# Down projections of two feed-forwards as seven products of quarters instead of eight, in a two-layer float32 kernel

## The chip, the cores and the metric

The kernel runs on one core of one Trainium2 chip. The metric is the device time of one execution in microseconds (us), as the median over runs. Engines are named PE (TensorE, the matmuls), DVE (VectorE), ACT (ScalarE), POOL (GpSimd) and SP (SyncE, whose queue starts all the DMAs of this kernel).

## The reference, cut to what matters

Two transformer layers follow each other on 1024 tokens of width 1024, all in float32. Each ends in a feed-forward with 2816 hidden units, which is 22 blocks of 128:

```python
# first layer (hybrid_layer)
gu = jnp.einsum('bsd,df->bsf', x, w_gu)
gate, up = gu[..., :FFN_HIDDEN], gu[..., FFN_HIDDEN:]
ffn = jnp.einsum('bsf,fd->bsd', jax.nn.silu(gate) * up, w_down)
return layer_norm(DEEPNORM_ALPHA * x + ffn, ln2_g, ln2_b)
# second layer (second_block)
h = rmsnorm(x, g_ffn_pre[l]) * (1.0 + scale_f) + shift_f
f = (jax.nn.silu(h @ w_gate[l]) * (h @ w_up[l])) @ w_down[l]
x = x + gate_f * rmsnorm(f, g_ffn_post[l])
```

What is at issue here is the last product of each, hidden (1024 tokens x 2816) times `w_down` (2816 x 1024). Before the feed-forward of the first layer stand three mixers (a gated one, a differential attention with 4 heads, a sparse attention whose keys are the top 256 of a score) and an output projection; before that of the second a stick-breaking attention and a pooling mixer. A vector of modulations for the second layer, silu(c) times `w_cond_2` (1024 x 6144), is computed beside the first layer's feed-forward.

## The kernel before, in words

**Precision.** A float32 operand x is held as two numbers of a shorter form, high and low: ACT copies x into `wh` (or `yh`), and POOL (for weights) or DVE (for activations) subtracts it from x into `wl` (or `yl`). Each product of two blocks is three matmuls, high x high, high x low and low x high, added up in one bank of PSUM (L546 to L548 for the down projections, L1878 to L1880 for gate and up). A matmul has a 128x128 stationary part and 512 columns that stream.

**Weights.** All weights come in units of 128x1024 numbers (512 KB) in one fixed order, `plan`. SP loads them into a ring of 3 buffers `raw` (L430), ACT and POOL split them into a ring of 5 pairs `wh`, `wl` (L478, L481 and L493, L498). `ahead(m)` says how many loads and splits may have been issued by the time unit m is used; `sp_feed`, `act_feed`, `pool_feed` issue up to that point, and each engine's queue runs strictly in order.

**The feed-forward of a layer** (`pe_ffn`, `act_ffn`, `pool_ffn`, `dve_ffn`, `sp_ffn`, called once per layer) has three stages:
- Early: the first 4 of the 22 hidden blocks, gate and up, as plain products (L520 to L522).
- Pairs: the other 18 blocks, 2 at a time, first gate (even q), then up (odd q). With tokens, inputs and columns halved, each q is a product of 2x2 quarters, which Strassen's scheme in Winograd's form makes from 7 products instead of 8: 18 x 7 products s of 12 matmuls. DVE makes the four sums of weights (`wdiff`, L460 to L465) and puts the 7 products together from the banks (L2011, L2020, L2022); for odd q it multiplies by the silu of the gate (L2018). The finished pair of hidden blocks lies in one of two buffers `hid`, and SP stores it to `qk_d` in DRAM, 2 transfers of 512 KB for each odd q (L2119). `BESIDE_LAST` brings the first 6 blocks back during the last pair. In the first layer DVE also adds up one part of the modulations in most products (L1675; its 256 KB of `w_cond_2` come through the buffers `early`, SP, L1685), and PE turns sums of 8 parts (L1645).
- Down: the 22 hidden blocks come back from DRAM in 4 chunks (`CHUNKS`: 6, 6, 6 and 4 blocks). For each chunk, each half n of the output columns and each block tb of 128 tokens, one bank takes 18 (or 12) matmuls, and DVE adds it to `res`, which holds all 1024x1024 outputs (L2069, L2075, L2077). That is 22 x 16 x 3 = 1056 matmuls per layer. The last chunk goes tb by tb, so that the norm behind it starts block by block (`after_block`, `after_half`). In the first layer `res` starts as the residual, which SP brings back once `res` is free (`sp_residual`).

**The attention of the first layer** (`pe_attend` and its like, 48 events and 7 places behind them) ran with no weights to feed: eight units of `w_out` were loaded beforehand and five of them split. DVE finishes the choice of keys (L1195 to L1209) and then takes maxima and sums for PE's logits (L1322, L1347).

Banks are handed out by rings; `ring(*bufs)` gives a new ring, and `prior(key)` is what freed a bank last.

## Time and profile before

| what | value |
|---|---|
| median of 3 runs | 2487.4 us (2480.76 to 2490.2) |
| the profiled execution | 2484.37 us |
| its span in the profile | 2482.2 us, 31284 instructions |
| PE busy | 2376.1 us (96%), 11999 matmuls |
| DVE, ACT, POOL busy | 1495.6, 962.7, 671.6 us |
| the chain that ended last | PE 79%, DVE 11%, DMA 4%, ACT 3%, issue 1%, POOL 1% |
| memory read and written | 197.36 and 59.82 MB, 104 GB/s over the span |

The stages of the feed-forwards in the trace: early 666 to 757 us, pairs 757 to 1122, down 1122 to 1373 in the first layer; early 1797 to 1889, pairs 1889 to 2233, down 2233 to 2474 in the second. The first layer's attention takes 345 to 574. A matmul's duration in the trace (389 ns) is that of one instruction from start to end; since several are under way at once, what counts is the distance from one start to the next.

### The profile page before, as it was taken

Reading aid. Unit: us, or ns where it says so; the run is one execution under the profiler, and the core shown is the slowest. Engines: PE = TensorE matmul, PEld = TensorE weight load, DVE = VectorE, ACT = ScalarE, POOL = GpSimd, SP = SyncE. Lnnn points to the kernel's source line nnn. Section 1 sums busy time; section 2 is a strip of 40 time slices with the busy share of each in tenths; the row PEclk is TensorE's granted clock in tenths of the full one; section 3 lists DMA queues with packets and bytes.
Section 4 is the critical chain, followed back from the end, with each engine's and each line's share of the span. In section 5 each row is a group of like instructions: output and inputs, shape, how many; then the busy total and the mean of one; then the engine's idle time right before and its main releaser. Section 6 shows DMA issues by size and latency. Waiting matters only on the chain.

```text
span 2482.2 us, 31284 instructions
## 1 busy us (share of the span) xinstructions
PE 2376.1 (96%) x11999; PEld 1922.5 (77%) x11999; DVE 1495.6 (60%) x2510; ACT 962.7 (39%) x1834; POOL 671.6 (27%) x382
## 2 busy tenths in 40 slices
PE   8999978889999999999999999999899999999998
PEld 6678866777888777777888777777688888888886
DVE  3588998662776777854226578773674555453225
ACT  3467837771222322232212355563533223231212
POOL 3013210000233545542222321110223445442220
PEclk9999988999999999999999999999999999999999
DMA  5026451214314454545332210001421322243333
GB/s 177 9 64 191 153 178 56 98 31 154 122 55 140 149 161 145 168 163 192 102 106 90 71 52 27 28 26 69 144 77 57 96 86 69 85 144 111 102 111 119
DMA packets 219980, 259.21 MB, mean 104 GB/s; under 512 B 16540, under 2 KB 150188, under 8 KB 219832
## 3 DMA queue, kind: packets, MB, share of 16 engines
q1 hardware_dynamic: 219832, 257.22, 31.7%
q8 instruction: 95, 1.56, 0.3%
q14 instruction: 53, 0.43, 0.1%
HBM read 197.36 MB, written 59.82 MB: 104 GB/s over the span
## 4 chain that ended last, share of the span: by engine, by line
PE 79%; DVE 11%; DMA 4%; ACT 3%; issue 1%; POOL 1%; SPq 0%; POOLq 0%; DVEq 0%; ACTq 0%
PE bank L546 10%; PE bank L548 10%; PE bank L547 10%; PE bank L1878 7%; PE bank L1879 7%; PE bank L1880 7%; PE bank L520 6%; PE bank L521 6%; PE bank L522 6%; PE bank L1387 2%; PE bank L2512 1%; DMA early<-in_w_cond 1%; DVE res L1322 1%; PE bank L2481 1%; PE bank L565 1%
## 5 line engine op out<-in xcount | busy, mean ns | idle before, releaser
L498 POOL TENSOR_TENSOR wl<-raw,wh 128x1024 fp32r<-128x1024 f32 x117 | 298.3, 2566 | 1333.0 <-ACT wh L481 1312.9
L546 PE MATMUL bank<-wh,yh 128*128 128x512 f32 x704 | 277.9, 395 | 5.5 <-DVE sum3l L1843 2.8
L547 PE MATMUL bank<-wl,yh 128*128 128x512 f32 x704 | 275.3, 391 | 0.0
L548 PE MATMUL bank<-wh,yl 128*128 128x512 f32 x704 | 275.3, 391 | 0.0
L481 ACT ACTIVATE wh<-raw 128x1024 fp32r<-128x1024 f32 x117 | 123.1, 1060 | 308.5 <-PE bank L548 291.5
L493 POOL TENSOR_TENSOR wl<-res,wh 128x512 fp32r<-128x512 f32 x144 | 197.9, 1397 | 151.0 <-ACT wh L478 130.3
L1878 PE MATMUL bank<-yh,wh 128*128 128x512 f32 x576 | 225.2, 391 | 0.0
L1880 PE MATMUL bank<-yh,wl 128*128 128x512 f32 x576 | 224.2, 389 | 0.0
L1879 PE MATMUL bank<-yl,wh 128*128 128x512 f32 x576 | 224.1, 389 | 0.0
L493 POOL TENSOR_TENSOR wl<-raw,wh 128x512 fp32r<-128x512 f32 x108 | 157.6, 1474 | 228.6 <-ACT wh L478 228.6
L520 PE MATMUL bank<-yh,wh 128*128 128x512 f32 x448 | 180.2, 402 | 8.3 <-DVE yl L583 8.3
L2077 DVE TENSOR_TENSOR res<-bank,res 128x512 f32<-128x512 f32 x96 | 65.6, 689 | 190.8 <-PE bank L548 190.7
L2011 DVE TENSOR_TENSOR res<-bank,res 128x512 f32<-128x512 f32 x144 | 99.6, 692 | 131.1 <-PE bank L1880 123.2
L522 PE MATMUL bank<-yh,wl 128*128 128x512 f32 x448 | 175.3, 391 | 0.0
L521 PE MATMUL bank<-yl,wh 128*128 128x512 f32 x448 | 175.1, 391 | 0.0
L546 PEld LDWEIGHTS bank<-wh,yh 128*128 128x128 f32 x704 | 133.0, 189 | 35.7 <-issue 4.6
L478 ACT ACTIVATE wh<-res 128x512 fp32r<-128x512 f32 x144 | 83.4, 623 | 194.7 <-DVE res L465 145.2
L548 PEld LDWEIGHTS bank<-wh,yl 128*128 128x128 f32 x704 | 132.9, 189 | 27.9
L547 PEld LDWEIGHTS bank<-wl,yh 128*128 128x128 f32 x704 | 133.1, 189 | 27.0
L1878 PEld LDWEIGHTS bank<-yh,wh 128*128 128x128 f32 x576 | 108.1, 188 | 29.8 <-issue 4.3
L1880 PEld LDWEIGHTS bank<-yh,wl 128*128 128x128 f32 x576 | 108.1, 188 | 22.7
L1879 PEld LDWEIGHTS bank<-yl,wh 128*128 128x128 f32 x576 | 108.1, 188 | 22.2
(345 smaller groups left out, 5385.9 us busy)
## 6 DMA issues: line engine op xcount, KB each, us to landing
early<-in_w_cond SPq DMA_DIRECT2D x96, 256.0 KB, 3.0
raw<-in_w_gu SPq DMA_DIRECT2D x44, 512.0 KB, 4.1
raw<-in_w_down SPq DMA_DIRECT2D x44, 512.0 KB, 3.6
raw<-in_w_in SPq DMA_DIRECT2D x40, 512.0 KB, 4.1
qk_d<-res SPq DMA_DIRECT2D x36, 512.0 KB, 4.2
raw<-in_w_gate SPq DMA_DIRECT2D x22, 512.0 KB, 4.2
raw<-in_w_up SPq DMA_DIRECT2D x22, 512.0 KB, 4.2
res<-in_x SPq DMA_DIRECT2D x16, 512.0 KB, 9.8
```

Of the source, the lines that this page charges most:

```text
L481: act.i.activation(wh[n % NU][:, :], raw_of(u)[:, :], ACT.Copy).then_inc(*av.up(("wh", u)))
L493: pool.i.tensor_tensor(wl[n % NU][:, half], src, wh[n % NU][:, half].bitcast(F32), ALU.subtract).then_inc(*po.up(("wl", u)))
L498: pool.i.tensor_tensor(wl[n % NU][:, :], raw_of(u)[:, :], wh[n % NU][:, :].bitcast(F32), ALU.subtract).then_inc(*po.up(("wl", u)))
L520: pe.i.matmul(bank[:, :], a, a_h[:, s], start=k == 0, stop=False)
L521: pe.i.matmul(bank[:, :], a, a_l[:, s], start=False, stop=False)
L522: last = pe.i.matmul(bank[:, :], b, a_h[:, s], start=False, stop=k == 7)
L546: pe.i.matmul(bank[:, 0:wide], xa, h[:, c:c + wide], start=k == 0, stop=False)
L547: pe.i.matmul(bank[:, 0:wide], xa, l[:, c:c + wide], start=False, stop=False)
L548: last = pe.i.matmul(bank[:, 0:wide], xb_, h[:, c:c + wide], start=False, stop=k == nk - 1)
L1878: pe.i.matmul(bank[:, :], h[:, c:c + 128], high[:, k, :], start=k == 0, stop=False)
L1879: pe.i.matmul(bank[:, :], h[:, c:c + 128], low[:, k, :], start=False, stop=False)
L1880: last = pe.i.matmul(bank[:, :], l[:, c:c + 128], high[:, k, :], start=False, stop=k == 3)
```

## The change

The same scheme of seven products now makes the down projection of the 18 later blocks. They go as 9 couples (blocks 2c and 2c+1 of them), which are the two halves of the inner dimension; the tokens are halved at 512 and the output columns at 512. The hidden side needs 7 operands for each couple, 4 as they are and 3 sums, all 128x512: DVE makes one (`third`), POOL the other three (`pool_parts`) right behind each odd q, and SP stores all seven (256 KB each) to `parts_d`. The weight side needs 7 operands too; three are quarters of `w_down`, and four are sums ("crossed weights"). These are made ahead: for the first layer by POOL beside the attention (`pool_cross`, 9 x 4 subtractions of 128x512, in the place of two of the `raw` buffers), for the second by DVE in odd q of its pairs (`dve_cross`, 9 x 4), each time loaded (1 MB) and stored (1 MB) by SP.

The down stage (`pe_down`) then runs 7 products, one after the other. A product i holds four banks open at once, one for each 128 of the 512 tokens, and goes over its 9 couples; an operand (i, c) is one 256 KB transfer of hidden numbers and half a unit "D" of weights, and serves 4 x 3 matmuls. 20 slots take the operands; SP loads 16 ahead, ACT and DVE split 8 ahead. DVE puts the products together in `res` with two sums `u_sum` and `v_sum` (`dve_down`). The 4 early blocks follow as plain products, tb by tb, as the last chunk did before. In matmuls: 7 x 9 x 4 x 3 + 4 x 16 x 3 = 756 + 192 = 948 per layer, where 1056 were.

```diff
-CHUNKS = [(0, 6), (6, 6), (12, 6), (18, 4)]
+N_EARLY, N_PAIR, N_COUPLE = 4, 18, 9
+N_OPERAND, N_HIDDEN, N_SLOT = 63, 71, 20
...
-            for a, k in CHUNKS:
-                for n in range(2):
-                    units += [("T", wd, j, 512 * n) for j in range(a // 2, (a + k) // 2)]
+            units += [("D", layer, i) for i in range((N_OPERAND + 1) // 2)]
+            for n in range(2):
+                units += [("T", wd, j, 512 * n) for j in range(N_EARLY // 2)]
...
+        def pool_cross():
+            for c in range(N_COUPLE):
+                pool.wait_ge(*cross_in[0].after(c))
+                for out_, x, y in cross(1):
+                    pool.wait_ge(*po.now())
+                    pool.i.tensor_tensor(out_, x, y, ALU.subtract).then_inc(*po.up(("cross", 1, c)))
...
         def sp_attend():
...
             for t in range(N_PLACES):
+                if t % 5 == 1 and t // 5 < N_COUPLE:
+                    sp_cross_in(1, t // 5)
+                if t % 5 == 4 and t // 5 < N_COUPLE:
+                    sp_cross_out(1, t // 5, po)
+                if t == 5 * N_COUPLE:
+                    sp.wait_ge(*cross_out[0].after(N_COUPLE - 1))
+                    sp_feed(project_released(N_PROJECT - 1))
...
+        LOAD_BESIDE = {0: range(0, 4), 1: range(4, 8), 2: range(8, 12), 4: range(12, 16), 5: range(16, 17)}
+        SPLIT_BESIDE = {3: range(0, 2), 4: range(2, 4), 5: range(4, 5), 6: range(5, 8)}
+        LOADS_AHEAD, SPLITS_AHEAD = 16, 8
...
+        def pool_parts(layer, q):
+
+            a11, a21, a12 = piece(q, 0, 0), piece(q, 0, 1), piece(q, 1, 0)
+            pool.wait_ge(*dv.after(("part", layer, 3, q)))
+            pool.i.tensor_tensor(a21, a11, a21, ALU.subtract).then_inc(*po.up(("part", layer, 4, q)))
+            pool.wait_ge(*dv.after(("hidden", layer, q, 6)))
+            pool.i.tensor_tensor(whole, third, a11, ALU.subtract).then_inc(*po.up(("part", layer, 2, q)))
+            pool.wait_ge(*po.now())
+            pool.i.tensor_tensor(first[1], a12, whole, ALU.subtract).then_inc(*po.up(("part", layer, 6, q)))
...
+            G["r"] = ring(*banks)
+            for i in range(7):
+                pe_down(layer, i)
+            G["r"] = ring(*banks[0:5])
...
+        def pe_down(layer, i):
+
+            for t in range(4):
+                key = ("down product", layer, i, t)
+                G["r"].open(key)
+                pe.wait_ge(*G["r"].prior(key))
+            for c in range(N_COUPLE):
+                o = N_COUPLE * i + c
+                u = down_unit(layer, o)
+                pe.wait_ge(*dv.after(("operand", layer, o)))
+                h, l = pe_unit(u)
...
+                for t in range(4):
+                    bank = uses.held["down product", layer, i, t]
+                    xa, xb_ = high[:, 128 * t:128 * t + 128], low_[:, 128 * t:128 * t + 128]
+                    pe.i.matmul(bank[:, :], xa, h[:, cols_], start=c == 0, stop=False)
+                    pe.i.matmul(bank[:, :], xa, l[:, cols_], start=False, stop=False)
+                    last = pe.i.matmul(bank[:, :], xb_, h[:, cols_], start=False, stop=c == N_COUPLE - 1)
...
+            if q % 2 and s == 5:
+                dve_part(layer, q)
             if s == 3:
+                dve.wait_ge(*part_stored(3, q // 2 - 1).after((layer, 3, q // 2 - 1)))
+                dve.wait_ge(*po.after(("part", layer, 2, q // 2 * 2 - 1)))
                 dve.i.tensor_tensor(third, bank[:, :], u, ALU.add).then_inc(*dv.frees(uses, key))
...
+                    if layer == 2 and q % 2 and s == 0:
+                        dve_cross(q // 2)
...
                 for s in range(7):
...
+                    if q and q % 2 == 0 and s in (0, 1):
+                        for i in ((4,), (2, 6))[s]:
+                            sp_part(layer, i, q - 1)
...
                     if layer == 1:
                         sp_mod(q, s)
+                    if q % 2:
+                        for i in {1: (0,), 4: (5,), 5: (3,), 6: (1,)}.get(s, ()):
+                            sp_part(layer, i, q)
...
+            for o in range(N_OPERAND):
+                dve_operand(layer, o + SPLITS_AHEAD)
+                if o % N_COUPLE == N_COUPLE - 1:
+                    dve_down(layer, o // N_COUPLE)
```

How it moves instructions is seen at three places. The first is SP's queue in the pairs of the first layer, from product s = 5 of an odd q into the even q behind it. `qk_d` and `parts_d` are the stores of the hidden numbers, `early` the loads of `w_cond`. Before:

```order
L1685 DMA early_128<-in_w_cond 128x512 [waits dve_done]
L2119 DMA qk_d<-res 128x1024
L1685 DMA early_129<-in_w_cond 128x512 [waits dve_done]
L2119 DMA qk_d<-res 128x1024
L1685 DMA early_128<-in_w_cond 128x512 [waits dve_done]
L1685 DMA early_129<-in_w_cond 128x512 [waits dve_done]
```

And now:

```order
L1758 DMA early_128<-in_w_cond 128x512 [waits dve_done]
L1918 DMA parts_d<-res 128x512
L1753 DMA vec_d<-macc_131 1x512
L1758 DMA early_129<-in_w_cond 128x512 [waits dve_done]
L1918 DMA parts_d<-res 128x512
L1918 DMA parts_d<-res 128x512 [waits pool_done]
L1758 DMA early_128<-in_w_cond 128x512 [waits dve_done]
L1918 DMA parts_d<-res 128x512 [waits pool_done] x2
L1758 DMA early_129<-in_w_cond 128x512 [waits dve_done]
```

The stores are seven smaller ones for each odd q, and three of them wait for POOL ahead of two loads of `w_cond`. The second place is POOL's queue behind an odd q, whose splits stood back to back before; now:

```order
L523 TENSOR_TENSOR wl_64<-raw_56,wh_59 128x512 [waits act_done]
L523 TENSOR_TENSOR wl_64<-res,wh_59 128x512 [waits dve_done]
L1929 TENSOR_TENSOR res<-res 128x512
L1931 TENSOR_TENSOR res<-res 128x512
L1933 TENSOR_TENSOR res<-res 128x512 [waits pool_done]
L523 TENSOR_TENSOR wl_65<-res,wh_60 128x512 [waits act_done]
L523 TENSOR_TENSOR wl_65<-res,wh_60 128x512
```

Three subtractions stand between the splits of one unit and the next. The third place is POOL's queue across the attention, where nothing stood before between the last split of `w_out` and the next stage; of the 9 groups that stand there now, the last is followed by the splits of the stage behind:

```order
L529 TENSOR_TENSOR wl_66<-raw_56,wh_61 128x1024 [waits act_done,raw_in2]
L1566 TENSOR_TENSOR cross_132<-cross_132 128x512 [waits pool_done,cross_in0]
L1566 TENSOR_TENSOR cross_132<-cross_132 128x512 [waits pool_done] x3
L1566 TENSOR_TENSOR cross_132<-cross_132 128x512 [waits pool_done,cross_in0]
L1566 TENSOR_TENSOR cross_132<-cross_132 128x512 [waits pool_done] x3
```

Each group of four waits for a load of 1 MB and works in place, so the four run one after the other.

## Rows read from the trace of the kernel before

**Rows 1.** The page, busy time of PE: us, share of the span, instructions.

```profile
PE 2376.1 (96%) x11999; PEld 1922.5 (77%) x11999; DVE 1495.6 (60%) x2510; ACT 962.7 (39%) x1834; POOL 671.6 (27%) x382
```

**Rows 2.** By stage: us, then PE, PEld, DVE, ACT, POOL busy, PEclk, DMA share, GB/s.

```profile
345.00:574.00 229.00, 181.83 (x1356) 151.77 (x1356) 166.88 (x498) 159.29 (x412) 5.10 (x2) 0.88 0.29 98
...
757.00:1122.00 365.00, 359.16 (x1538) 285.06 (x1537) 265.71 (x339) 110.22 (x183) 178.33 (x122) 1.00 0.50 156
1122.00:1373.00 251.00, 247.92 (x1096) 204.91 (x1097) 101.14 (x143) 51.64 (x66) 67.55 (x27) 0.99 0.34 119
...
1889.00:2233.00 344.00, 343.72 (x1517) 284.28 (x1515) 179.61 (x231) 111.78 (x184) 163.83 (x122) 1.00 0.29 92
2233.00:2474.00 241.00, 239.95 (x1056) 198.04 (x1056) 88.17 (x116) 46.89 (x58) 49.65 (x19) 1.00 0.33 111
```

**Rows 3.** What PE waited for: us in total, times, longest.

```profile
PE bank L1297 <- DVE st L1322: 21.9, 7, 16.6
...
PE bank L1645 <- DVE macc L1675: 5.8, 2, 3.3
PE bank L546 <- POOL wl L498: 3.2, 7, 0.7
...
PE bank L546 <- DVE sum3l L1843: 2.8, 2, 2.2
```

**Rows 4.** PE in order of time, from the first layer's pairs into its down stage.

```profile
1121.59 0.39 PE L1880 MATMUL bank<-sum4h,wl 128*128 128x512 f32 x1
1124.20 0.50 PE L546 MATMUL bank<-wh,yh 128*128 128x512 f32 x1 [2.22 <-DVE sum3l L1843]
...
1126.83 0.63 PE L547 MATMUL bank<-wl,sum2h 128*128 128x512 f32 x1
1127.25 0.63 PE L548 MATMUL bank<-wh,sum2l 128*128 128x512 f32 x1
```

**Rows 5.** Durations in ns (min/median/max) of 128x512 operations of DVE and POOL.

```profile
L2018 DVE TENSOR_TENSOR res<-res x72: 691/693/1984, 787.4 to 2239.7; 128x512 f32<-128x512 f32 x72
...
L2011 DVE TENSOR_TENSOR res<-bank,res x144: 691/692/695, 766.8 to 2239.0; 128x512 f32<-128x512 f32 x144
...
L493 POOL TENSOR_TENSOR wl<-res,wh x144: 1269/1297/1762, 740.5 to 2206.8; 128x512 fp32r<-128x512 f32 x144
```

**Rows 6.** DVE by line, whole span: count, busy us, mean ns, idle time before.

```profile
L2018 DVE TENSOR_TENSOR res<-res 128x512 f32<-128x512 f32 x72 | 66.0, 916 | 2.5
```

**Rows 7.** DVE by line, 345 to 574 us, forms together; columns as in Rows 6.

```profile
L1347 DVE SCALAR_TENSOR_TENSOR res<-res,st 128x128 f32<-128x128 f32 (+7 forms) x32 | 26.2, 819 | 1.1
...
L1440 DVE SCALAR_TENSOR_TENSOR osb<-osb,st,sg 128x128 f32<-128x128 f32 x32 | 8.8, 346 | 0.1
```

**Rows 8.** POOL in order of time, 330 to 360 us.

```profile
345.12 5.10 POOL L498 TENSOR_TENSOR wl<-raw,wh 128x1024 fp32r<-128x1024 f32 x2 [19.88 <-ACT wh L481]
```

**Rows 9.** DVE in order of time, around those two operations of POOL.

```profile
345.15 2.87 DVE L1201 SCALAR_TENSOR_TENSOR junk<-res,cand,junk 128x512 bf16<-128x512 f32 x1
348.06 2.71 DVE L1205 SCALAR_TENSOR_TENSOR score<-score,cand,junk 128x512 f32<-128x512 f32 x1
350.80 0.69 DVE L1209 SCALAR_TENSOR_TENSOR score<-score,nd 128x512 f32<-128x512 f32 x1
...
353.64 0.88 DVE L1201 SCALAR_TENSOR_TENSOR junk<-res,cand,junk 128x640 bf16<-128x640 f32 x1
```

**Rows 10.** What DVE waited for, 757 to 1122 us: us in total, times, longest.

```profile
DVE macc L1675 <- DMA early<-in_w_cond: 27.9, 23, 5.1
DVE res L2011 <- PE bank L1880: 22.9, 22, 4.7
DVE macc L1672 <- DMA vec_d<-macc: 20.6, 4, 5.9
```

**Rows 11.** DMA issues: operation and count, KB each, median us from issue to landing.

```profile
early<-in_w_cond SPq DMA_DIRECT2D x96, 256.0 KB, 3.0
```

**Rows 12.** The fastest 5 us of transfers in the first down stage, columns as in Rows 2.

```profile
1140.00:1145.00 5.00, 5.00 (x24) 4.13 (x23) 0.00 (x0) 0.00 (x0) 0.00 (x0) 1.00 1.03 415
```

424 lines of the change are left out of this document (251 added, 173 removed).

## The prediction

> **What bounds the kernel now.** I read the page first: PE is busy 2376.1 of 2482.2 us [rows 1], so the time is PE's work plus its few gaps. The table by stage says where [rows 2]: in the pairs of the second layer and in both down stages PE is busy all but 0.3 to 3.1 us, at a granted clock of 0.99 to 1.00. DVE, ACT and POOL are busy less than half of a down stage. Three places are less clean. In the first layer's attention PE is busy 181.8 of 229 us. In the first layer's pairs 365 us pass for the same products that take 344 us in the second; the modulations are made beside them, and DVE is busy 265.7 us. Third, PE pays a little at the entry of a down stage. The list of PE's waits puts numbers on them [rows 3]: 21.9 us for DVE's maxima (16.6 in one piece), 5.8 us for sums of modulations, 3.2 and 2.8 us for splits of weights and hidden numbers. So matmuls taken out of a down stage come off the time, if nothing else in that stage becomes longer than the shorter PE work, and the preparations elsewhere must not widen the gaps there.
>
> **The price of a matmul.** The second layer's down stage has 1056 of them in 239.95 us [rows 2]: 0.2272 us each. Its durations are not the price, since they overlap.
>
> **PE's work.** Per layer 1056 - 948 = 108 matmuls go, 216 in both, of the same shape. 216 x 0.2272 = **-49.1 us**. Nothing else is on PE's path in these stages, so all of it counts, provided that the rest keeps up:
>
> - One operand is 12 matmuls, 2.73 us. Per operand DVE splits 128x512 (0.69 us, as a subtraction of that size [rows 5]) and POOL half a unit (1.30 us [rows 5]). ACT copies both; it was busy 46.9 us in the stage before [rows 2], with 22 hidden blocks and 22 units per layer, and now has 35.5 of each, some 76 us of about 215. DVE adds 4 to 12 combining operations per product of 24.5 us, at most 12 x 0.69 = 8.3 us beside 6.2 us of splits. The first layer's product with 12 is the fullest, at 60%. The splits run 8 operands (22 us) ahead and a product's four banks are needed again only after the next product. I cost this at nothing. If POOL and DVE hold each other up, the cover is those 22 us.
> - Transfers: 256 KB of hidden numbers and 256 KB of weights per 2.73 us is 192 GB/s. The trace moved 119 and 111 GB/s in these stages [rows 2] but 415 GB/s over 5 us of one of them [rows 12]. In the first layer 4 MB of residual come on top, about 10 us at that rate, against the 16 operands (44 us) of loads ahead. Nothing, with 0 to +5 us for the range.
> - SP's queue issues two transfers per operand instead of one per block and one per unit. It waits for a slot freed 4 operands earlier and is far ahead of its use. Nothing.
>
> **The entry of a down stage.** Before, PE stood 2.2 us for the low half of hidden blocks and then ran at a distance of 0.42 us between matmuls for a while [rows 4]. Now it waits for the last banks of the pairs, one combining operation of 0.69 us [rows 5], while the first operands are split three products earlier. A gap of about 1 us stays, the slow stretch may too. I take 0 with -5 to +3 us for both layers.
>
> **The crossed weights of the first layer.** 36 subtractions of POOL at 1.30 us [rows 5], 47 us, run between some 360 and 540 us, where POOL did nothing. They cost through DVE. When POOL's two splits ran at 345.12 us [rows 8], DVE operations with two inputs in SBUF took 2.87 and 2.71 us, and 0.69 and 0.88 us for the same size or a larger one behind them [rows 9]; each lost about 2 us to one POOL operation of 2.55 us. Operations that read a bank never did this: 695 ns at most in 144 [rows 5]. So what counts are DVE's two-input operations here: 32 and 32 [rows 7] and some 15 for the choice of keys. In the pairs, with POOL busy 48% of the time [rows 2], one such operation took 916 ns on average against a median of 693 [rows 5, 6], 0.22 us more. Here POOL will be busy about 25% of the time, so 0.12 us x 79 = 9 us of DVE's time. DVE is on the path for part of this stage only (21.9 us of waits, most before 383 us), and the groups start there back to back. I take **+6 us**. Below it could be 0; above, each POOL operation hits one of DVE on the path: 36 x 1.3 x 0.8 = 37 us. The value is near the low end, since that is where the average over 72 operations puts it. Where the three last units of `w_out` are loaded, at place 45 of 55, some 40 us are left until the stage behind needs them. Nothing.
>
> **The seven operands beside the pairs, first layer.** POOL's 27 subtractions (35 us) fit in its queue: the splits behind them are 5 units, 10 products, ahead. DVE's 9 additions of 0.69 us do too. The place that costs is SP's queue. Behind an odd q POOL must first split a unit whose second half is a difference that DVE makes only after that q's last product: combine, multiply, part, then three of the differences, about 5 us, then ACT, the split and one subtraction, some 8 us after PE has left that q; the other two subtractions end near 11 us. SP waits for them ahead of two loads of `w_cond`, which it issued at about 6 and 9 us before. A load lands 3.0 us after its issue [rows 11], so the part of product s = 2 has its numbers about 2 us late, and that of s = 4 about as much. DVE already waits 27.9 and 20.6 us for such transfers here and only 22.9 us for PE [rows 10], so its slack is thin, but it has the rest of 14 products to catch up, and PE waits for DVE directly only at the sums of 8 parts, 5.8 us so far [rows 3]. Nine times 2 to 4 us would be 18 to 36 us if all of it reached PE. I take **+5 us**, nearer to the low end because of those 5.8 us; below 0.
>
> **The same in the second layer, and its crossed weights.** 45 more operations of DVE at 0.69 us are 31 us in a stage where DVE is busy 179.6 of 344 us and PE had 0.3 us without work [rows 2]. There are no loads of `w_cond`. **+1 us**, 0 to +3.
>
> **The sum** against the profiled execution: 2484.4 - 49.1 + 0 + 6 + 5 + 1 = 2447.3 us. The median of the runs shown is 3.0 us above that execution, so the median should be about **2450 us**.
>
> **Rivals.**
>
> *PE runs slow in the new loop* (slower). The new loop changes the bank every three matmuls, where 12 to 18 went to one bank before. If PE paused at these changes and the clock fell to its lower level, a matmul would cost 0.42 us as in the short stretch after the entry [rows 4] instead of 0.227. All 1896 at that level would be +366 us. It decides from 49.1 / 0.193 = 254 slow matmuls on, 13% of them; half of the product loops' 1512 slow gives 2450 + 146 = 2596 us. Against it: bank changes every 12 matmuls in the second layer's pairs leave the clock at 1.00 and no gap [rows 2], and nothing in the new loop waits between its groups of three. Chance 0.03. The Trainium skill (TensorE: Matmul & The Clock Gate, "A second HAM failure mode: psum-queue depth-cycling") reports a kernel whose cycling through banks in each iteration made PE idle briefly between groups, so that its clock went up and down. By that rule this rival would be the forecast; the row on the pairs, which cycle banks too, speaks against it.
>
> *Transfers starve the down stages* (slower). The products need 63 x 0.524 = 33.0 MB per layer. At the 119 GB/s seen there [rows 2] that takes 278 us instead of 172, +106 per layer: 2660 us. It decides once the rate stays below some 168 GB/s, where 25 us per layer are lost again. For it: transfers of 2 KB rows, half of them from memory that was just written. Against: 415 GB/s [rows 12]. Chance 0.03.
>
> *The first layer's pairs become paced by DVE and SP.* 4 us for each of the 9 odd q and what the locks add reach PE: +31 over my +5, 2481 us. For it: the thin slack [rows 10]. Chance 0.07.
>
> *POOL's subtractions sit on the attention's path.* +20 over my +6: 2470 us, up to 2481 at the bound. For it: DVE is the bound at the start of that stage. Chance 0.10.
>
> **How the numbers follow.** My forecast has 0.77. The range: the low end is 2487.4 - 49.1 with the entries gained, and nothing lost, 2433, of which I take 2436; the high end takes in the attention rival and the other upper bounds that may come together, to 2476. About 2 in 10 stay outside, with the two slow rivals, the pairs' rival and some of my own case. 0.5% is 12.4 us, about what a measurement of this kernel can tell from no change; below 2475 counts as faster. Faster: 0.77 and most of the attention case, 0.86. Same: the pairs' rival and the rest, 0.08. Slower: 0.06.
>
> **What would show it.** In the trace after: down stages of about 215 to 220 us each with PE busy in all but 1 or 2 us, 948 matmuls at 0.227 us, and 190 GB/s. In the attention, L1347 with a mean above 819 ns and the stage 229 us plus 4 to 10. In the first layer's pairs, longer waits of DVE for `early` and 365 us plus 2 to 8; in the second layer's, 344 to 346. POOL's three subtractions should end 9 to 12 us after the odd q. The prediction is wrong if a down stage has gaps in PE or a clock below 0.95, or if either preparation stage grows by over 15 us.

## The result and the profile after

The changed kernel takes 2498.95 us (median of 7 runs, 2496.6 to 2503.59), the kernel before 2481.59 us in the same session (7 runs): a ratio of 1.0065, 95% interval 1.005 to 1.0079. It is **slower**, by 17.4 us between the medians, where a median of 2450 us was forecast. The page of the profiled execution (2496.6 us; its span is 2494.8) answers to [rows 1]:

```profile
span 2494.8 us, 31779 instructions
...
PE 2341.4 (94%) x11783; PEld 1888.7 (76%) x11783; DVE 1680.2 (67%) x2646; ACT 1018.9 (41%) x1960; POOL 851.4 (34%) x500
...
HBM read 244.55 MB, written 92.85 MB: 135 GB/s over the span
...
PE 71%; DVE 16%; DMA 5%; POOL 3%; ACT 2%; issue 2%; SPq 0%; DVEq 0%; ACTq 0%; POOLq 0%
```

The matmuls did go: 11999 - 11783 = 216 records, and PE is busy 34.7 us less. Yet PE's share of the chain fell from 79 to 71%. Something else now sets the end in several places. The table by stage, columns as in [rows 2]: attention, pairs and down of the first layer, pairs and down of the second.

```profile
345.00:586.00 241.00, 183.58 (x1357) 151.53 (x1355) 183.20 (x497) 159.09 (x413) 57.98 (x38) 0.88 0.49 174
768.00:1164.00 396.00, 370.26 (x1540) 290.48 (x1538) 268.63 (x347) 107.39 (x185) 210.00 (x146) 0.96 0.51 159
1171.00:1379.00 208.00, 205.84 (x900) 169.96 (x901) 158.98 (x163) 71.10 (x107) 86.14 (x37) 0.99 0.58 201
1914.00:2258.00 344.00, 343.78 (x1517) 284.44 (x1515) 201.65 (x275) 109.15 (x186) 192.83 (x146) 1.00 0.49 162
2265.00:2486.00 221.00, 218.85 (x948) 180.33 (x947) 147.24 (x142) 75.72 (x116) 77.24 (x33) 0.98 0.54 182
```

Inside the seven products PE waits for nothing, and the stages move 182 to 201 GB/s. The pairs of the first layer are the surprise: 396 us for PE's 370, while DVE is busy 268.63 us, hardly more than the 265.71 before. PE's own busy time there grew too, from 359.16 [rows 2] to 370.26 us for the same products, at a granted clock of 0.96 where it was 1.00.

To add the stages up I took them between the first matmuls of successive stages, read from PE in order of time. The same table serves all runs below (us; "entry" is from the last matmul of the pairs to the first of the down stage, "down" from there to the next stage):

| kernel | start to out projection | pairs 1 | entry 1 | down 1 | pairs 2 | entry 2 | down 2 |
|---|---|---|---|---|---|---|---|
| before | 574.5 | 364.3 | 2.6 | 230.8 | 342.5 | 1.0 | 239.9 |
| changed | 585.9 | 394.9 | 7.3 | 208.2 | 342.5 | 7.2 | 221.3 |
| difference | +11.4 | **+30.6** | +4.7 | -22.6 | 0 | +6.2 | -18.6 |

The differences add to +11.7; with +1.0 between the first down stage and the second layer's pairs this is the spans' 12.6 to within 0.1. The medians lie 17.4 us apart, so this pair of profiles holds some 5 us less than the medians show; the changed kernel's reached the out projection early (585.9 us, where the median of thirteen profiles with the same code up to there is 589.0). What PE waited for, all of the span, answers to [rows 3]:

```profile
PE bank L1330 <- DVE st L1355: 27.0, 12, 16.6
PE bank L1718 <- DVE macc L1748: 25.7, 11, 4.5
PE bank L2010 <- DVE res L2116: 13.7, 2, 6.9
...
PE bank L577 <- DVE res L2232: 4.3, 2, 2.2
```

The sums of modulations (5.8 us before) now cost 25.7. With the 11.1 us that PE is busy longer this makes up the growth of the pairs, 31.0 us by these windows: about a third of it is not waiting but matmuls at a lower clock behind the waits. The last row is a small wait of 2.2 us in each layer, between the seventh product and the early blocks. A new and larger wait stands at both entries. Here is the first, PE and then DVE in order of time (start, duration, in brackets the idle time before and its releaser):

```profile
1163.56 0.39 PE L1959 MATMUL bank<-sum4h,wl 128*128 128x512 f32 x1
1170.89 0.76 PE L2010 MATMUL bank<-wh,yh 128*128 128x512 f32 x1 [6.94 <-DVE res L2116]
```

```profile
1158.38 0.69 DVE L1900 TENSOR_TENSOR yl<-landing,yh 128x512 fp32r<-128x512 f32 x1 [1.86 <-ACT yh L1895]
...
1162.34 2.07 DVE L1730 TENSOR_TENSOR macc<-macc 128x48 f32<-128x48 f32 x1
...
1166.45 2.05 DVE L2123 TENSOR_TENSOR res<-res 128x512 f32<-128x512 f32 x1
1168.54 0.69 DVE L1923 TENSOR_TENSOR res<-res 128x512 f32<-128x512 f32 x1
1169.15 0.69 DVE L1900 TENSOR_TENSOR yl<-landing,yh 128x512 fp32r<-128x512 f32 x1
1169.94 0.69 DVE L2116 TENSOR_TENSOR res<-bank,res 128x512 f32<-128x512 f32 x1
```

The down stage's first product asks for four banks at once, and one is that of the very last pair product. The operation that frees it (1169.94) stands in DVE's queue behind the operations of the products before it and behind splits that wait for ACT and a landing. Two operations ahead of it took 2.07 and 2.05 us; beside both POOL was splitting a weight unit (2.40 us from 1161.95, 2.35 from 1165.61). The first of the two takes 0.19 us in the kernel before, with nothing of POOL's beside it. PE's clock falls with the gap: the windows at the second entry show 1.00, 0.69, then 0.50 (the 1.2 GHz level), 0.90, 1.00.

```profile
2250.00:2257.00 7.00, 7.00 (x33) 5.79 (x32) 4.11 (x7) 4.77 (x8) 1.72 (x2) 1.00 0.98 358
2257.00:2264.50 7.50, 0.78 (x4) 0.32 (x2) 7.19 (x8) 3.22 (x5) 5.22 (x3) 0.69 1.02 395
2264.50:2269.00 4.50, 4.44 (x11) 3.51 (x12) 4.50 (x4) 0.00 (x0) 3.39 (x3) 0.50 1.05 397
2269.00:2274.00 5.00, 5.00 (x21) 4.12 (x20) 1.35 (x3) 1.12 (x2) 0.00 (x0) 0.90 0.89 332
```

In the pairs, SP's and DVE's largest waits, 768 to 1167 us:

```profile
SPq L1918 <- POOL res L1929: 57.6, 8, 7.7
```

```profile
DVE macc L1748 <- DMA early<-in_w_cond: 63.5, 25, 5.9
DVE macc L1745 <- DMA vec_d<-macc: 17.1, 4, 4.3
```

That looks like the forecast's mechanism at full size: SP waits 57.6 us for POOL ahead of loads of `w_cond`, and DVE waits 63.5 us for these (27.9 before). The experiments say that this reading names one way of several.

### The profile page after: what moved, and what is told of

It is laid out like the page before. It is cut to its first block, busy times and chain, and to the rows that moved or that the text cites. A ratio compares the mean times of both kernels' runs of the same rounds, so it can differ in the third digit from the quotient of the medians.

```text
span 2494.8 us, 31779 instructions
## 1 busy us (share of the span) xinstructions
PE 2341.4 (94%) x11783; PEld 1888.7 (76%) x11783; DVE 1680.2 (67%) x2646; ACT 1018.9 (41%) x1960; POOL 851.4 (34%) x500
## 4 chain that ended last, share of the span: by engine, by line
PE 71%; DVE 16%; DMA 5%; POOL 3%; ACT 2%; issue 2%; SPq 0%; DVEq 0%; ACTq 0%; POOLq 0%
PE bank L551 6%; PE bank L553 6%; PE bank L552 6%; PE bank L1957 5%; PE bank L1959 5%; PE bank L1958 5%; PE bank L577 5%; PE bank L578 5%; PE bank L579 5%; PE bank L2010 5%; PE bank L2012 5%; PE bank L2011 5%; DMA early<-in_w_cond 3%; PE bank L1420 2%; POOL wl L523 2%
## 5 line engine op out<-in xcount | busy, mean ns | idle before, releaser
L529 POOL TENSOR_TENSOR wl<-raw,wh 128x1024 fp32r<-128x1024 f32 (+1 forms) x145 | 356.6, 2465 | 1039.2 <-ACT wh L511 1019.2
L511 ACT ACTIVATE wh<-raw 128x1024 fp32r<-128x1024 f32 (+1 forms) x145 | 152.0, 1055 | 300.9 <-PE bank L2012 225.7
L1900 DVE TENSOR_TENSOR yl<-landing,yh 128x512 fp32r<-128x512 f32 x112 | 157.0, 1441 | 81.0 <-ACT yh L1895 81.0
L2010 PE MATMUL bank<-wh,yh 128*128 128x512 f32 x408 | 160.8, 394 | 13.7 <-DVE res L2116 13.7
L2116 DVE TENSOR_TENSOR res<-bank,res 128x512 f32<-128x512 f32 x144 | 99.6, 692 | 109.4 <-PE bank L1959 99.1
L577 PE MATMUL bank<-wh,yh 128*128 128x512 f32 x400 | 159.9, 400 | 6.3 <-DVE res L2232 4.3
L2011 PE MATMUL bank<-wl,yh 128*128 128x512 f32 x408 | 160.3, 393 | 0.0
L2012 PE MATMUL bank<-wh,yl 128*128 128x512 f32 x408 | 160.2, 393 | 0.0
L578 PE MATMUL bank<-wl,yh 128*128 128x512 f32 x400 | 157.4, 393 | 0.0
L579 PE MATMUL bank<-wh,yl 128*128 128x512 f32 x400 | 157.1, 393 | 0.0
L1748 DVE SCALAR_TENSOR_TENSOR macc<-early,cc,macc 128x512 f32<-128x512 f32 x84 | 85.5, 1018 | 70.0 <-DMA early<-in_w_cond 63.5
```

What stands on the lines that cost most here:

```text
L529: pool.i.tensor_tensor(wl[n % NU][:, 0:w], raw_of(u)[:, 0:w], wh[n % NU][:, 0:w].bitcast(F32), ALU.subtract).then_inc(*po.up(("wl", u)))
L577: pe.i.matmul(bank[:, 0:wide], xa, h[:, c:c + wide], start=k == 0, stop=False)
L2010: pe.i.matmul(bank[:, :], xa, h[:, cols_], start=c == 0, stop=False)
L2011: pe.i.matmul(bank[:, :], xa, l[:, cols_], start=False, stop=False)
L2012: last = pe.i.matmul(bank[:, :], xb_, h[:, cols_], start=False, stop=c == N_COUPLE - 1)
```

## The experiments

### First group: banks, SP's stores, POOL's subtractions

**Banks.** The ring of the seven products begins with the three banks that the pairs don't use and goes on with those used longest ago; the ring behind it begins with the banks of the product before last.

```
-            G["r"] = ring(*banks)
+            k = G["r"]
+            old = [k.bufs[(k.n + j) % 5] for j in range(5)]
+            G["r"] = ring(*banks[5:8], *old)
...
-            G["r"] = ring(*banks[0:5])
+            G["r"] = ring(*old[1:5], old[0])
```

> The changed kernel, but the ring of banks for the seven products starts with the three banks that the pairs do not use and then the longest free ones, so that the first product no longer needs the bank of the pairs' last product; the ring behind it starts with the banks of the product before last. Bank theory: PE's gap of 7.3 us at each entry of a down stage came only from that one bank, freed late by DVE; the gaps fall to about 1 us, the slow stretch behind them and the 2.2 us in front of the early blocks go too: 12 to 17 us less than the changed kernel, about 2484. Rival: the operands themselves are split too late, PE waits for them instead, and no more than 4 us go: about 2496.

Measured: 2478.14 us against 2486.34 of before, ratio 0.9967 (0.9956 to 0.9978). Entries 0.2 and 0.2 us, down stages 205.8 and 216.4, with the clock at 1.00 throughout:

```profile
1169.50:1340.70 171.20, 171.20 (x757) 141.75 (x755) 134.67 (x119) 66.74 (x96) 82.26 (x36) 1.00 0.70 238
...
2253.80:2424.90 171.10, 171.10 (x757) 141.70 (x755) 121.92 (x102) 66.70 (x96) 81.83 (x36) 1.00 0.63 215
```

These two windows are the seven products of each layer; no distance between two matmuls' starts is above 0.3 us in them. The theory stands. It gave more than the 14.1 us of the gaps: another 2.4 and 4.9 us in the down stages. Of these, 1.7 and 2.6 us are the matmuls at the lower clock behind the entries. The rest lies at the early blocks. With the edit's second half the distance between the two matmuls there is 1.89 us in place of 2.54 in each layer, and in the second layer seven slow matmuls behind it (1.5 us) are gone. Its pairs (397.5) are as long as the changed kernel's. Four profiles have the change's code throughout the pairs (the changed kernel, this run and two below), and they took 394.9 to 397.5 us: a difference of 3 us in one profile is not much more than this spread.

**SP's stores later.** The three stores that wait for POOL move from the first two products of an even pair to behind the `w_cond` load of the third.

```
-                    if q and q % 2 == 0 and s in (0, 1):
-                        for i in ((4,), (2, 6))[s]:
-                            sp_part(layer, i, q - 1)
...
                         sp_mod(q, s)
+                    if q and q % 2 == 0 and s == 2:
+                        for i in (4, 2, 6):
+                            sp_part(layer, i, q - 1)
```

> The changed kernel, but SP's three stores that wait for POOL stand behind the loads of w_cond of product s = 2 of the even q, instead of ahead of those of s = 0 and s = 1. Queue theory: the loads were late because SP stood before them waiting for POOL; DVE's wait for them falls from 63.5 us back towards 28, PE's wait for the sums of parts from 25.7 towards 6, and the first layer's pairs shrink from 395 us by 20 to 28: total about 2475. Load theory (rival): DVE is late from its own added work and from being held up by POOL; the stage loses no more than 6 us: total 2493 or more.

Measured: ratio 1.008 (1.0062 to 1.0098), pairs 399.5 us. SP's wait for L1929 fell from 57.6 to 7.7 us and DVE's for `early` from 63.5 to 35.7, as expected, and the time did not fall. DVE now waited 34.8 us for `vec_d` (17.1 in the changed kernel), and 7.7 us for POOL itself. The queue theory in its simple form falls, unless the row store explains it (second group).

**Without POOL's subtractions, and without those of the attention.** Two runs that leave work out:

```
-                if o % 14 == 13:
-                    pool_parts(layer, o // 7)
```

> POOL's three subtractions behind each odd q are left out (three of the seven operands then hold other numbers), their stores stay in their places in SP's queue and wait only for DVE's last hidden quarter. Queue theory: like the run with the later stores, the first layer's pairs lose 20 to 28 us, since SP no longer waits for POOL; the rest of what this run gains beyond that one is what the subtractions cost through DVE, 0 to 6 us. Load theory: this run gains 20 us or more and the run with the later stores next to nothing.

Measured, one run: 2477.64 us, pairs 373.1. This takes out 21.8 of the 30.6 us, but two causes with them, since SP's stores don't wait for POOL either (three of the seven operands hold other numbers in this run).

```
-            pool_cross()
...
-            sp.wait_ge(*done.after(("cross", layer, c)))
+            sp.wait_ge(*(cross_in[0].after(c) if layer == 1 else done.after(("cross", layer, c))))
```

> POOL's 36 subtractions beside the attention are left out (four of the weight operands of the first layer's down projection are then plain quarters); the 1 MB loads and stores around them stay, each store waiting for its load. Lock theory: POOL's subtractions hold up DVE, and the start of the output projection comes back from 586 us to 574.5 to 577. Rival: the 18 MB of transfers and their place in SP's queue delay the heads' loads and the results' stores; the start stays at 583 or later.

Measured, one run: 2488.4 us; the out projection starts at 576.6. DVE's lines in the attention (L1380 was L1347 before the change, L1377 was L1344), in the changed kernel and then here:

```profile
L1380 DVE SCALAR_TENSOR_TENSOR res<-res,st 128x128 f32<-128x128 f32 (+7 forms) x32 | 34.8, 1088 | 1.1
L1377 DVE SCALAR_TENSOR_TENSOR st<-st,cand 128x1 f32<-128x1 f32 x32 | 11.9, 371 | 1.1
```

```profile
L1380 DVE SCALAR_TENSOR_TENSOR res<-res,st 128x128 f32<-128x128 f32 (+7 forms) x32 | 26.2, 818 | 1.1
...
L1377 DVE SCALAR_TENSOR_TENSOR st<-st,cand 128x1 f32<-128x1 f32 x32 | 7.0, 220 | 1.1
```

The transfers stayed and only POOL's 36 subtractions went, so it is they that hold DVE's operations up: 8.6 + 4.9 = 13.5 us on these two lines, of which 9 to 12 reached the out projection (576.6 against 585.9 in the changed kernel's profile and 589.0 in the median). L1380 is back at the 819 ns of [rows 7]. A marker that scatters less is the last product for the logits (L1297 before, L1330 now). It starts at 541.4 us here, at 539.9 and 540.7 in the two profiles whose attention is that of before, and at 551.2 to 554.7 in the thirteen that have the subtractions.

### Second group: is it the queue or the subtraction?

**Crosses later in the attention.**

```
-                if t % 5 == 1 and t // 5 < N_COUPLE:
-                    sp_cross_in(1, t // 5)
...
+                w = t - 12
+                if w >= 0 and w % 4 == 0 and w // 4 < N_COUPLE:
+                    sp_cross_in(1, w // 4)
```

> The changed kernel with one edit: the nine groups of crossed weights beside the first attention start at its twelfth place and come every fourth place, instead of starting at once and every fifth. Nothing is left out. Theory (GpSimd's subtractions of two SBUF operands and VectorE's operations of two SBUF operands hold each other up, and 8.5 of attention's 11.4 us were lost beside the first three groups, where VectorE ends last; later TensorE ends last): the first product of the out projection starts 6 to 10 us earlier than in the changed kernel (576 to 580 against 585.9), the total is 6 to 10 us lower, about 2491. Rival (the cost goes with the number of subtractions, wherever they stand): no shift, within 3 us of the changed kernel. Rival (the groups now end too late, and w_out's load is late): first product later than 586.

Measured: ratio 1.0053 (1.0036 to 1.007), out projection at 583.9. In thirteen profiles with the code up to there as the change has it, it starts between 585.9 and 592.1, median 589.0; so the gain is 2 to 5 us and not the 6 to 10 expected. The last product for the logits starts at 547.8 us, 3.4 to 6.9 before the thirteen and 6.4 behind the run without subtractions. L1380 still took 1046 ns on average. As far as one profile can tell, the place is worth a part of the cost, and between half and two thirds of it goes with the number of subtractions.

**Stores later and row store earlier.** As the second run above, and

```
-            if h % 8 == 7 and h > 8:
+            if h % 8 == 5 and h > 8 and h < N_PART:
                 sp_mod_row(h // 8 - 1)
```

> The changed kernel with two edits: SP's three stores that wait for GpSimd move from the first and second place of an even pair to behind the w_cond load of its third (as in the run that moved these stores alone), and the row store vec_d<-macc comes two parts earlier in SP's order (at the sixth part of a group of eight in place of the eighth). Nothing is left out. Queue theory, mended (the stores' move alone gained nothing because the row store, which VectorE's next group waits for, then stood behind them and behind a weight load that waits for GpSimd's split): macc's wait for vec_d falls from 34.8 (there; 17.1 in the changed kernel) to under 5 us, the wait for early stays near 36, the first layer's pairs take 375 to 385 us against 394.9, the total is 10 to 20 lower, about 2485. Lock theory (what costs is GpSimd's subtractions beside VectorE's work, and VectorE's waits for them): the pairs stay at 392 to 400.

Measured: ratio 1.006 (1.0045 to 1.0075), pairs 396.5. DVE's wait for `vec_d` did go; that for `early` came back at 67.2 us. A wait taken from one place turned up at the next: the mended queue theory misses too.

**SP free of POOL, POOL as it was.** The stores that waited for POOL store `third` and wait for DVE. What else relied on these stores waits for them or for POOL directly: DVE ahead of writing `third`, ACT ahead of writing `first[1]`. Three operands hold other numbers in this run too.

```
-            return (piece(q, 0, 0), piece(q, 1, 0), whole, third, piece(q, 0, 1), piece(q, 1, 1), first[1])[i]
+            return (piece(q, 0, 0), piece(q, 1, 0), third, third, third, piece(q, 1, 1), third)[i]
...
-                         3: dv.after(("part", layer, 3, q))}.get(i, po.after(("part", layer, i, q))))
+                         3: dv.after(("part", layer, 3, q))}.get(i, dv.after(("hidden", layer, q, 6))))
```

> The changed kernel with SP's three stores of an even pair left where they are, but storing the sum that VectorE made in place of the three differences that GpSimd makes, and waiting for VectorE alone; GpSimd still makes its three subtractions at the same place of its own queue (their results are not stored, so the down products' operands are not the reference's). It is the counterpart of the run without these subtractions, whose pairs took 373.1. Queue theory (SP's 57.6 us of waits for GpSimd hold back the loads of w_cond, and these VectorE): first layer's pairs 372 to 380 us, macc's wait for early near 27, total 15 to 22 lower, about 2480. Lock theory (the subtractions themselves, on GpSimd, hold up VectorE's operations of two SBUF operands): pairs stay above 388. Between: each has its share, to be read from the pairs' length between 373 and 395.

Measured: ratio 1.0074 (1.0059 to 1.0089), pairs 399.4. This is the run that decides: with no store of SP's waiting for POOL the pairs are as long as ever, and without the subtractions they are 26 us shorter. (DVE's waits for POOL come to 9.3 us in all. Its wait for `early` fell to 39.1 us, but that for `vec_d` rose from 17.1 to 33.0.) SP's waits for POOL did not go but moved. These are its waits for POOL's splits ahead of a weight load, in the changed kernel and then here:

```profile
SPq L105 <- POOL wl L523: 71.2, 25, 4.7
```

```profile
SPq L105 <- POOL wl L523: 121.4, 26, 14.5
```

The trace shows by what way. SP, POOL and DVE of this run, in order of time:

```profile
867.70 2.03 SPq L1758 DMA_DIRECT2D early<-in_w_cond  x2
877.43 1.00 SPq L459 DMA_DIRECT2D raw<-in_w_gu  x2
878.48 7.74 SPq L1758 DMA_DIRECT2D early<-in_w_cond  x4
```

```profile
864.59 1.28 POOL L523 TENSOR_TENSOR wl<-raw,wh 128x512 fp32r<-128x512 f32 x1 [9.69 <-ACT wh L507]
...
867.08 1.74 POOL L1929 TENSOR_TENSOR res<-res 128x512 f32<-128x512 f32 x1
868.78 1.75 POOL L1931 TENSOR_TENSOR res<-res 128x512 f32<-128x512 f32 x1
870.60 1.29 POOL L1933 TENSOR_TENSOR res<-res 128x512 f32<-128x512 f32 x1
871.85 4.25 POOL L523 TENSOR_TENSOR wl<-res,wh 128x512 fp32r<-128x512 f32 x3
876.06 1.30 POOL L523 TENSOR_TENSOR wl<-raw,wh 128x512 fp32r<-128x512 f32 x1
```

```profile
873.66 1.28 DVE L1748 SCALAR_TENSOR_TENSOR macc<-early,cc,macc 128x512 f32<-128x512 f32 x1
...
884.26 1.61 DVE L1748 SCALAR_TENSOR_TENSOR macc<-early,cc,macc 128x512 f32<-128x512 f32 x2 [5.57 <-DMA early<-in_w_cond]
```

POOL's three subtractions push its splits back. SP's next weight load (L459) waits for the split of the raw tile that it overwrites, at 876.06; the `w_cond` load stands behind that weight load in SP's order, and DVE waits 5.57 us for it. So SP waits for POOL by a second way, that no store shows. And POOL had stood idle for 9.69 us just before.

**Row store earlier in the kernel before.** A control.

> The kernel before the change, with the row store vec_d<-macc two parts earlier in SP's order, and nothing else. A control for the run that moves it in the changed kernel: it shows what of that gain the kernel before would have had too. Theory: macc's 20.6 us of waits for vec_d (4 times) go, but TensorE waited only 5.8 us in all for macc there, so the first layer's pairs shorten from 364.3 by 0 to 6 us and the total by as much. Rival (VectorE's waits in the pairs of the kernel before were all covered): no change, within 1 us.

Measured, one run: 2483.07 us; pairs 360.9 against 364.3. 3.4 us, within what was expected; the total doesn't show it, since the out projection started 5.5 us later in this profile (580.1), all but 0.8 us of it behind the last product for the logits.

### Third group: orders

**Subtractions first in POOL's order.**

```
-                pool_feed(operand_unit(layer, o))
                 if o % 14 == 13:
                     pool_parts(layer, o // 7)
+                pool_feed(operand_unit(layer, o))
```

> The changed kernel with one edit in GpSimd's order: the three subtractions of a couple stand ahead of the low half of the weights of the product after the couple, not behind it. Nothing is left out. What is known by now: with SP's stores freed of their waits for GpSimd the first layer's pairs still took 399.4 us, without the subtractions 373.1. Loop theory (GpSimd does its subtractions and then the low halves of three operands before that of the next raw tile; SP's weight load waits for that tile, the w_cond load stands behind it in SP's order, VectorE waits for w_cond, TensorE for VectorE's macc): in the trace GpSimd sat idle 9.5 us waiting for the high half just ahead of that place, with the inputs of the subtractions there for at least 4 us, so with this edit they fall into idle time: pairs 376 to 386 us against 394.9, PE's waits for macc fall from 25.7 to 5 to 15, total 10 to 18 lower, about 2485. Lock theory (VectorE's operations of two SBUF operands are slowed by GpSimd's wherever they stand): pairs stay at 390 to 398.

Measured: ratio 1.0034 (1.0022 to 1.0047), pairs 392.0, against the changed kernel's 1.0065 an improvement of about 8 us, of which the profile finds 2.9 in the pairs and 1.6 and 1.4 at the entries. DVE's wait for `early` fell from 63.5 to 22.2 us, below the 27.9 of before, but PE still waited 26.0 us for `macc`. The pairs lie where the rival was expected (390 to 398), and DVE's busy time says why: 288.1 us in the pairs for 268.2 in the changed kernel, with two operations more. In the new order the subtractions run while DVE is at work and stretch its operations. In the second layer the same edit made DVE busy 219.2 us for 201.1, and the pairs stayed at 342.5.

**`w_cond` ahead of the weight load in SP's order.**

```
-                    if (7 * q + s) % 2:
-                        sp_feed(operand_unit(layer, 7 * q + s))
                     if layer == 1:
                         sp_mod(q, s)
+                    if (7 * q + s) % 2:
+                        sp_feed(operand_unit(layer, 7 * q + s))
```

> The changed kernel with one edit in SP's order: in a product's slot the w_cond load (and the row store vec_d<-macc) stands ahead of the weight load, not behind it. Nothing is left out. Loop theory: w_cond's loads no longer wait for GpSimd's low halves by way of the weight load of their own slot, though still behind that of the slot before and behind the stores that wait for GpSimd: pairs of the first layer 380 to 390 us against 394.9, total 5 to 15 lower. Rival (weight loads now stand behind SP's waits for VectorE's parts and come late themselves): a new wait of the splits for raw, pairs above 395. Lock theory: no change, 393 to 397.

Measured: ratio 1.0056 (1.0041 to 1.0071), pairs 391.5: 3.4 us shorter. Less than expected (380 to 390).

**All edits together:** banks, both orders above, SP's stores behind the third product, the row store two parts earlier.

> The changed kernel with the banks' order of the earlier run (2478.1 against 2486.3 of before), GpSimd's subtractions first, w_cond loads ahead of weight loads, the three stores that wait for GpSimd behind the weight load's place of the third product, and the row store two parts earlier. Nothing is left out. Loop theory: first layer's pairs 366 to 378 us (the kernel before: 364.3), both entries 0.2 us, total 2455 to 2468, faster than both kernels. Lock theory: pairs 390 or more, total about 2478.

Measured: 2465.53 us against 2483.03, ratio 0.9932 (0.9913 to 0.9951). Pairs 383.2: 11.7 us of the 30.6 come back where single edits gave 3 at most. The forecast of 366 to 378 was still too low. What is left shows in DVE's lines at an odd pair's end, here beside POOL's at 856.80 (1.27 us), 860.22 (1.26) and 861.56 (1.59):

```profile
856.03 0.69 DVE L1923 TENSOR_TENSOR res<-res 128x512 f32<-128x512 f32 x1
856.82 1.79 DVE L1748 SCALAR_TENSOR_TENSOR macc<-early,cc,macc 128x512 f32<-128x512 f32 x1
...
860.24 1.78 DVE L1748 SCALAR_TENSOR_TENSOR macc<-early,cc,macc 128x512 f32<-128x512 f32 x1
861.95 1.75 DVE L489 TENSOR_TENSOR res<-raw,raw 128x512 f32<-128x512 f32 x1
```

Each of the three long ones starts beside a subtraction of POOL's and takes about 1 us more than the 0.75 (L1748) or 0.69 us (L489) that it takes alone. DVE's commonest operation with two inputs in SBUF, all 84 of it in the pairs, in the kernel before, the changed kernel, the run without POOL's subtractions and this one:

```profile
L1675 DVE SCALAR_TENSOR_TENSOR macc<-early,cc,macc 128x512 f32<-128x512 f32 x84 | 86.0, 1024 | 34.6 <-DMA early<-in_w_cond 27.9 <-DVE res L2011 0.5
```

```profile
L1748 DVE SCALAR_TENSOR_TENSOR macc<-early,cc,macc 128x512 f32<-128x512 f32 x84 | 85.5, 1018 | 70.0 <-DMA early<-in_w_cond 63.5
```

```profile
L1748 DVE SCALAR_TENSOR_TENSOR macc<-early,cc,macc 128x512 f32<-128x512 f32 x84 | 84.4, 1004 | 33.6 <-DMA early<-in_w_cond 26.8 <-DVE macc L1722 0.5
```

```profile
L1748 DVE SCALAR_TENSOR_TENSOR macc<-early,cc,macc 128x512 f32<-128x512 f32 x84 | 100.2, 1192 | 46.5 <-DMA early<-in_w_cond 38.8
```

So the stretching hardly plays a part in the pairs of the changed kernel (1018 ns against 1004 without the subtractions); there the subtractions cost by the queues. It appears once they stand first: 64 of the 84 then run beside some operation of POOL's, against 48 before and in the changed kernel.

**The same with SP's stores and row store in their old places.**

> As the run of all edits together, but SP's three stores and its row store stay where the change put them: banks' order, GpSimd's subtractions first, w_cond loads ahead of weight loads. Nothing is left out. It tells whether the stores' places matter once the loop by way of the weight load is gone. Loop theory: with the subtractions done in GpSimd's idle time the stores at the first and second product wait for them 2 to 4 us in place of up to 7.7, pairs 370 to 382, total 2460 to 2470. Rival (the stores' waits still hold the loads of w_cond): over 8 us longer than the run of all edits.

Measured: ratio 0.9955 (0.994 to 0.997), 2471.95 us, pairs 389.5: 6.3 us above the run of all edits, where 370 to 382 was expected and the rival asked for over 8 us. So the places of the stores and of the row store together do matter, once the other ways are open; DVE's wait for `vec_d` is 24.1 us here and none with all edits.

### Fourth group: the subtractions on DVE

```
-                if o % 14 == 13:
+                if o % 14 == 13 and layer == 2:
                     pool_parts(layer, o // 7)
...
+            if layer == 1 and q % 2 and s == 6:
+                dve_parts(layer, q)
```

`dve_parts` holds the three subtractions of `pool_parts`, issued on DVE.

> The changed kernel with one edit: in the first feed-forward the three subtractions of a couple are VectorE's, behind the last product of the couple's second pair, and GpSimd has none (in the second they stay GpSimd's). Nothing is left out. VectorE gets 24 more operations of 0.69 us, 16.6 us, and GpSimd's 32 us of them go. Theory (a GpSimd subtraction costs more than itself: VectorE's operations beside it take 1.75 in place of 0.75 us, VectorE waits for its result, and the low halves and with them SP's weight and w_cond loads stand behind it): pairs of the first layer 376 to 386 us against 394.9, total 8 to 18 lower, about 2486. Rival (VectorE's chain through macc is what bounds these pairs, so 16.6 us more of work for it are worse than what they replace): pairs 395 to 405. Rival (only SP's waits mattered): as the run without the subtractions, 373.

Measured: ratio 1.0033 (1.0021 to 1.0044), pairs 386.2, 8.7 us shorter than the changed kernel's, although DVE has 24 more operations of 0.69 us. The rival that DVE's work is the bound (395 to 405) falls.

> The run of all edits together (2465.5 us, pairs 383.2), but with the first feed-forward's subtractions on VectorE in place of earlier on GpSimd. Nothing is left out. Theory: with the queues already in order what is left of GpSimd's subtractions is the stretched VectorE operations, about three by 1 us for a couple, seen in that run's trace; VectorE's own take 2.1 us for a couple. Pairs 376 to 383, total 2458 to 2466. Rival (VectorE bounds): pairs 384 to 392, total up to 8 higher.

Measured: **2459.3 us** against 2481.48, ratio 0.9903 (0.9887 to 0.992), pairs 378.9. It is the fastest of all and beats both kernels. L1748's mean is 983 ns again.

> As the run before it, but SP's three stores stay at the first and second product of an even pair, since VectorE's results are there by then. Nothing is left out. Theory: SP waits under 1 us for each, pairs within 3 us of the run before it. Rival (the row store and the loads of w_cond suffer from any store there): 4 us or more above it.

Measured, one run: 2462.43 us, pairs 378.3: the stores' places no longer matter when nothing in them is late.

## Why the prediction was wrong

**The matmuls taken out: right.** -49.1 us was forecast. With the entries mended the two down stages and their entries take 205.8 + 216.4 + 0.4 = 422.6 us, against 230.8 + 239.9 + 3.6 = 474.3 before: -51.7 us, of which 48.5 are inside the stages and 3.2 at the entries. Transfers, the combining operations, splits and the bank changes after every three matmuls cost nothing inside the seven products, as argued; the two rivals on a slow clock there and on starved transfers are out. Not counted was the wait in front of the early blocks (2.2 us in each layer). The rule of the Trainium skill that was weighed (TensorE: Matmul & The Clock Gate, "A second HAM failure mode: psum-queue depth-cycling") does not bite in this loop: the granted clock is 1.00 over the seven products of both layers in the run with the other banks.

**The entries: the step "it waits for the last banks of the pairs, one combining operation of 0.69 us" failed.** The operation is 0.69 us long, but it stands last in a queue: 6.9 and 6.8 us of waiting, then 8 and 13 matmuls 0.34 to 0.56 us apart. I priced the operation and not its place in DVE's order, with splits of the next stage put between. Forecast 0 (at most +3); measured, against the run with the other banks, 14.1 us of gaps, 4.3 of slow matmuls behind them and 3.0 in front of and behind the start of the early blocks. Against the kernel before, down stages and entries together gave -30.3 instead of -49.1.

**The attention: right mechanism, term too small.** +6 forecast, +11.4 in the profile. By the last product for the logits it is 11 to 15 us (551.2 to 554.7 against 539.9 and 540.7), and without the subtractions it is back (541.4). L1380's mean rose by 0.27 us where I took 0.12 for each operation. The average over 72 operations of the pairs was a poor donor; the one pair of operations that had shown 2 us each [rows 9] was the better warning.

**The first layer's pairs: the largest failure, +5 forecast, +30.6 measured.** The rival "become paced by DVE and SP" named the size to within 6 us (+31 over my +5, so 36) and got 0.07. I had argued that PE waits for DVE only at the sums, 5.8 us so far, and that DVE could catch up in the rest of 14 products. But a load for part h + 2 is issued only when part h is done, into one of two buffers, so a late load makes the next one late as well. That DVE's idle time was no slack for this reason is my reading; no run has more buffers. What the trace shows is that DVE's waits for `early` rose from 27.9 to 63.5 us, the top of the 18 to 36 us that I had given for the case that all of it reached PE, and that PE's waits for `macc` rose by 19.9. A second part stood nowhere in my sum: PE was busy 11.1 us longer, by matmuls at the lower clock behind those waits. And the path named, SP's stores, was only one of several. Freed of its stores' waits alone SP gained nothing (pairs 399.4). What the runs show instead, for the 30.6 us:

- 8.8 us stay when POOL's subtractions go (373.1). Left by then are DVE's 9 additions and the added stores and their waits; which of them it is wasn't tried.
- 21.8 us come with the subtractions. In the changed kernel they act by SP's waits: for its stores, and for POOL's delayed splits, which hold up a weight load and the `w_cond` load behind it. DVE's own operations are hardly longer there (268.2 us busy against 265.7 without the subtractions). With the subtractions first in POOL's order it is the other way round: fewer waits for loads, and DVE busy 20 us longer.
- 11.7 us of the 30.6 come back by order alone, in four edits together (383.2), and 16.0 with the subtractions on DVE besides (378.9). Not all of this need belong to the 21.8: the row store's edit gave 3.4 us in the kernel before as well.
- No single edit gave more than 3.4 us of it, apart from the subtractions moved to DVE (8.7): the ways run beside each other, and closing one shows the next. How the 21.8 us divide among the stores and the weight loads is not settled, since they don't add.

**The second layer's pairs:** forecast +1, measured 0. The same subtractions of POOL and even more additions of DVE are there. What is missing is the modulations: the loads of `w_cond`, DVE's work on them and the sums that PE waits for. This is the best control in the profile, and shows that the subtractions cost nothing without these; it doesn't tell the loads from DVE's work on them.

**The signs by which it was to be judged** worked: the pairs grew by over 15 us, PE had gaps at the entries, and L1380 rose. POOL's three subtractions were to end 9 to 12 us after the odd q. In the second layer they end 8.6 to 11.3 us after it, in the first 12.7 to 17.6, the last couple left out. The high end of 2476 missed by 23 us because some 20 us at the entries had a range of 3, and because the pairs went to their rival's size while the attention took twice its term. Against the forecast's 2447.3 us the profiled execution is 49.3 longer, mainly by 25.6 in the first layer's pairs, 18.8 in the down stages and their entries, and 5.4 up to the out projection. The pairs and the attention both hang on POOL's added work, so their chances should not have been taken as separate.

Open: the 14.6 us by which the best version's pairs are still longer than those of before, and the attention's 11. More than two buffers for `w_cond` weren't tried.

## What to carry to other kernels

Price a wait by what stands ahead of the releasing operation in its engine's queue, and not by that operation: the last bank of one stage should never be among the first that the next one asks for. An engine that is idle a third of the time beside double-buffered transfers, as DVE was here, may have no slack; look at what each of its waits waits for before counting idle time as cover. Count the slower matmuls behind a wait too: here they were a third of what the pairs lost. When work is added to an "idle" engine, follow every queue that waits for its other work (here a split that frees a tile, that lets a load go, in front of another load), and when one edit gives nothing, try the set before dropping the theory. Moving the added work into a quiet stretch of its own engine can put it beside another engine's operations that it stretches, so look at both engines' busy time after such an edit.

## What the runs showed that I had not expected

- The same operation was cheaper for the whole on the busier engine: 24 subtractions of 0.69 us on DVE in place of 1.3 us on POOL shortened the pairs by 8.7 us alone, and by 4.3 us in the kernel where the queues were in order.
- POOL held up even DVE's smallest operations with two inputs in SBUF: beside the subtractions 128x1 (L1377) went from 220 to 371 ns on average, and 128x48 (L1730) took 2.07 us beside a split of 2.40 us, against 0.19 us with POOL idle (L1657 in the kernel before).
- A gap of 7 us in PE cost 1.7 and 2.6 us more behind it, by the lower clock (0.50 in the window after the second one). Behind the two gaps of 2.2 us in front of the early blocks the matmuls ran at full pace in one layer and seven of them slowly in the other.
- Up to the out projection, thirteen profiles with the same code there differ by 6 us (585.9 to 592.1), while the second layer's pairs took 342.5 us in every one.
